# Attention heads on TensorE: the next head's probabilities are turned in front of the last head's products with the values

## The reference, cut to what matters

```
o_cmp = einsum('bgrqc,bgcd->bgrqd', p_cmp, v_cmp)              # compressed keys
o_slc = einsum('bgrqk,bgqkd->bgrqd', p_s, vs...)               # selected blocks
p_w   = safe_softmax(where(mask_w, s_w, -inf))
o_win = einsum('bgrqk,bgkd->bgrqd', p_w, vw)                   # window
return gb[..., 0:1] * o_cmp + gb[..., 1:2] * o_slc + gb[..., 2:3] * o_win
```

## Time and profile before

| what | value |
|---|---|
| median of 3 timed runs | 1402.15 us (1400.98 to 1402.82) |
| profiled execution | 1403.39 us, its span 1401.6 us |
| TensorE busy | 1336.2 us (95%) |
| VectorE busy | 787.1 us (56%) |
| ScalarE busy | 660.6 us (47%) |
| GpSimd busy | 39.5 us (3%) |
| HBM read and written | 429.40 MB and 1.05 MB |

### The profile page before, as it was taken

One profiled execution on the slowest core, in us unless ns is written; L12 is line 12 of the kernel. 1 busy time (PEld: TensorE's weight loads), 2 busy tenths in 40 slices (PEclk: granted clock), 3 DMA queues, 4 the chain that ended last, 5 costly groups with the idle time before them and its releaser, 6 DMA issues.

```text
span 1401.6 us, 19436 instructions
## 1 busy us (share of the span) xinstructions
PE 1336.2 (95%) x7580; PEld 1003.3 (72%) x7580; DVE 787.1 (56%) x864; ACT 660.6 (47%) x772; POOL 39.5 (3%) x97
## 2 busy tenths in 40 slices
PE   7999999998998898999999999999999999999996
PEld 7987888887986676777676766676666667666652
DVE  6855655545856858874376643367644266744332
ACT  5546543435645746763365532356542256633221
POOL 7000000001000000000000000000000000000000
PEclk9999999999999989999999999999999999999999
DMA  8453555554642035999999989999999999999996
GB/s 345 155 177 109 197 197 187 180 181 150 205 174 103 1 112 220 341 368 422 421 421 421 421 321 421 421 420 421 421 373 422 420 420 421 421 359 421 421 421 285
DMA packets 59993, 431.70 MB, mean 308 GB/s; under 512 B 6656, under 2 KB 6656, under 8 KB 7808
## 3 DMA queue, kind: packets, MB, share of 16 engines
q1 hardware_dynamic: 59760, 429.95, 77.3%
q10 hardware_dynamic: 144, 0.52, 0.1%
HBM read 429.40 MB, written 1.05 MB: 307 GB/s over the span
## 4 chain that ended last, share of the span: by engine, by line
PE 78%; DMA 13%; DVE 4%; ACT 4%; issue 1%; POOL 0%; SPq 0%; POOLq 0%; DVEq 0%; ACTq 0%
PE bank L1553 19%; PE bank L1555 19%; PE bank L1554 19%; DMA raw<-in_moe 12%; PE bank L2061 6%; PE bank L2082 6%; PE bank L1929 2%; DVE w_lo L1458 1%; ACT w_hi L855 1%; PE bank L2008 1%; PE bank L2109 1%; PE bank L1912 1%; PE bank L1903 1%; DMA raw<-in_wts 1%; PE bank L2016 1%
## 5 line engine op out<-in xcount | busy, mean ns | idle before, releaser
L1458 DVE TENSOR_TENSOR w_lo<-raw,w_hi 128x2048 fp32r<-128x2048 f32 x130 | 295.8, 2290 | 235.7 <-ACT w_hi L855 235.4
L855 ACT ACTIVATE w_hi<-raw 128x2048 fp32r<-128x2048 f32 x130 | 248.1, 1918 | 255.4 <-DMA raw<-in_moe 222.8
L1553 PE MATMUL bank<-w_hi,ht_hi 128*128 128x512 f32 (+1 forms) x768 | 303.1, 395 | 0.9 <-DVE ht_lo L989 0.9
L1555 PE MATMUL bank<-w_hi,ht_lo 128*128 128x512 f32 (+1 forms) x768 | 296.9, 387 | 0.0
L1554 PE MATMUL bank<-w_lo,ht_hi 128*128 128x512 f32 (+1 forms) x664 | 255.8, 385 | 0.0
L957 DVE TENSOR_TENSOR w_lo<-raw,w_hi 128x2048 fp32r<-128x2048 f32 x73 | 166.7, 2290 | 110.5 <-ACT w_hi L531 110.3
L531 ACT ACTIVATE w_hi<-raw 128x2048 fp32r<-128x2048 f32 x74 | 141.5, 1919 | 95.8 <-PE bank L1555 92.9
L1553 PEld LDWEIGHTS bank<-w_hi,ht_hi 128*128 128x128 f32 x768 | 144.7, 188 | 44.8 <-issue 13.7
L1555 PEld LDWEIGHTS bank<-w_hi,ht_lo 128*128 128x128 f32 x768 | 144.6, 188 | 30.1
L2061 PE MATMUL bank<-raw,xb 128*64 128x256 f32 x1280 | 147.1, 381 | 0.0
L1554 PEld LDWEIGHTS bank<-w_lo,ht_hi 128*128 128x128 f32 x664 | 125.2, 189 | 23.2
(11 more groups left out here) (339 smaller groups left out, 1568.5 us busy)
## 6 DMA issues: line engine op xcount, KB each, us to landing
raw<-in_moe SPq DMA_DIRECT2D x247, 1024.0 KB, 15.0
more<-in_moe SPq DMA_DIRECT2D x89, 1024.0 KB, 16.1
raw<-in_wts SPq DMA_DIRECT2D x71, 1024.0 KB, 4.8
xs<-in_x SPq DMA_DIRECT2D x2, 512.0 KB, 4.0
out<-xn SPq DMA_DIRECT2D x4, 256.0 KB, 2.0
pk<-in_packed SPq DMA_DIRECT2D x1, 517.0 KB, 8.4
g1b<-in_norm_ffn ACTq DMA_DIRECT2D x1, 512.0 KB, 6.0
gfb<-in_norm_final SPq DMA_DIRECT2D x1, 512.0 KB, 20.1
```

What stands on the lines that cost most here:

```text
L855: a(w_hi[:, hi_order(n) % SPLIT, :], slot_raw(n), ACT.Copy).then_inc(s_hi, 1)
L1458: v.tensor_tensor(slot_lo(n), slot_raw(n), w_hi[:, hi_order(n) % SPLIT, :].bitcast(F32), ALU.subtract).then_inc(s_lo, 1)
L1553: mm(out_, sh, mh, start=first, stop=False)
L1555: return mm(out_, sl, mh, start=False, stop=last)
```

## The change

In every step n the call of `head_transpose(n)` goes from behind `head_out(n - 1)` to in front of it. No instruction is added or taken away, and ScalarE's and VectorE's lists stay as they are.

```diff
         for n in range(2 * HB):
             if n % 2 == 0 and 4 <= n + 2 < 2 * HB:
                 pair_scores(n + 2)
+            head_transpose(n)
             if n:
                 head_out(n - 1)
-            head_transpose(n)
             if n % 2 == 0 and n >= 4:
                 pair_turned((n - 4) // 2)
         head_out(2 * HB - 1)
```

## The result

The changed kernel takes 1388.1 us (1386.9 to 1389.0, 4 runs) against 1401.89 of the kernel before beside it. The ratio is 0.9901, with a 95% interval from 0.9884 to 0.9918. The forecast was 1393.9, the range 1391.0 to 1397.5: faster, as forecast, but by 13.8 us instead of 8.3.

The account below looks back on a forecast made before the run. TensorE was taken to bound wide steps through its wait for ScalarE's copy, a VectorE-ScalarE ring narrow ones. 0.44 + 4.9 + 0 + 0.67 + 1.5 + 0.8 = 8.3 us off 1402.15 gave 1393.9 us, range 1391.0 to 1397.5.

Parts of the forecast that it names:

- first step: Products of step 0 wait for copied values; the turn of step 1 now lies in that wait: gain 0.44 us.
- wide even steps: Wide pairs fall from 5.00 to 4.30 us as the copy is hidden: 7 x 0.70 = 4.9 us.
- narrow steps: Gain 0 us: a ring without TensorE sets the pace, 3.03 us a pair or 4.11 with the splits.
- entry at step 24: Entry into the ring with the splits: step 24's copy no longer waits for its turn, gain 0.67 us.
- small ones: Remainder at changes between wide and narrow steps, between 0 and 1.5 us, taken as 0.8.
- last steps: From step 29's products on, two copies and the turn of step 30 leave the path: 1.5 us.
- the ring: VectorE and ScalarE, without TensorE, set the pace in narrow steps: 3.03 us a pair, 4.11 with the splits.
- The rule on weight loads: Loads pulled past a waiting instruction would cost 0.8 us of gain in all; the trace shows none.
- rivals 1, 3 and 4: Ring binds wide steps, 1397.0 us (0.17); turn delays coefficients, 1407.5 (0.03); waits replaced or already overlapped, 1402 (0.04).
- The clock: TensorE's clock, 0.51 from 492.50 to 500.50 us before, was expected to fall again, at an unknown place.
- Rival 2: Clock stays up in the last steps and projection: 10.7 us gain, 1391.5 us; chance 0.14.
- Carried to the end: Behind the loop, the expert weight stream starts earlier by the same amount, so the gain counts in full.

Follow-up runs that it names:

- first comparison: The changed kernel (every turn in front of the products) against the kernel before: 1388.1 us against 1401.89, ratio 0.9901.
- no_copy_wait: Kernel before, but products of step n read step n - 1's turned probabilities and wait for that copy alone: loop 60.40 us, whole 1608 us.
- narrow_only: Changed kernel with the turn in front of the products in narrow steps alone: 1395.8 us, ratio 0.9978 to the kernel before, loop 65.79 us.
- second comparison: The same changed kernel and kernel before, both unedited, measured again: 1388.9 us against 1399.3, ratio 0.9932.
- split_behind: Changed kernel with the two halves of the weight slot split behind the loop: 1385.4 us, ratio 0.9911 to the kernel before, loop 55.72 us.
- before_split_behind: Kernel before with the two halves of the weight slot split behind the loop: 1392.9 us, ratio 0.9962 to the unedited one, loop 64.58 us.

## Why the prediction was wrong

The main mechanism held: the copies left TensorE's path. The size was too small by 2.1 us in the loop, by two terms of the sum, and behind the second of them stands a bound that I had read wrongly. The first comparison added 3.4 us that aren't in the loop. Those put the time below the range: with the loop's 10.4 us alone it would have been 1391.8 us, inside it.

| step, as predicted | predicted | measured in the loop |
|---|---|---|
| first step | 0.44 | 0.45 |
| wide even steps | 7 x 0.70 = 4.9 | 1.00 + 0.89 + 1.02 - 0.02 + 0.90 + 0.88 + 0.99 = 5.7 |
| narrow steps | 0 | 0.06 a pair within a stretch, counted in the next row |
| entry at step 24, and small ones | 0.67 + 0.8 | 0.80 + 0.19 + 0.05 + 0.49 + 0.81 + 0.17 = 2.5 |
| last steps | 1.5 | 1.74 |
| sum | 8.3 | 10.4 |

(The measured ones are the differences of the distances between the scores of one pair and the next.)

- *Wide even steps* is a failed term. TensorE's own time in a pair is 4.10 us, not 4.30. I corrected the drain and the turned rows by estimates; what I missed is that products that wait pay for their weight load in full afterwards (0.11 us), shown by no_copy_wait, and 0.06 of order. The last 0.03 are within my estimate of the drain. One of the seven steps, 16, gave nothing: its turn waits 0.48 us for exponentials in the changed kernel, and the chain that ended last reaches it through the ring. So the term was wrong by 0.2 a pair and one pair too many.
- *The rule on weight loads* I turned the wrong way round, as something that could take from the gain. In the changed kernel the load at 436.67 us starts 0.11 us ahead of its matmul; in the kernel before the load at 440.90 us doesn't pass the waiting instruction. Together the two make the gain larger. The Trainium skill, "TensorE: Matmul & The Clock Gate", section "Step-by-step: what each phase is for", says that TensorE pulls weight loads ahead of running matmuls; the row at 436.67 us agrees.
- *Small ones*, with the entry at step 24, is the other failed term: 1.5 us predicted, 2.5 measured. Its cause is a wrong reading: "in narrow steps TensorE isn't the bound". In the kernel before it was, with its uncovered copies, and their wait was no slack; what the change could take was the distance down to the ring. Inside the stretch this is 0.06 us a pair, so the 0 of the narrow term was nearly right by luck. At the changes of shape it is more: narrow_only alone gives 0.8 us in the first narrow stretch and 0.84 at step 24. I had taken the copy of step 11, which shows no idle time, for all copies; those of even steps had waited for their turn.
- *The ring* has 2.97 us in narrow pairs, near the 3.03 that I had read off TensorE's own period, and 4.10 us with the splits, where it did bind before (4.11). Right were also the statement that a turn can't hold its products back by more than its length, and that the coefficients' wait stays small (2.0 us). So rivals 1, 3 and 4 fell. (The 4.19 us of rival 1 was the distance at the change from narrow to wide; the next one, between wide pairs, was 4.99, and is 3.93 now.)
- *The clock* fell and came back as I forecast, at 0.51 for 7 us, 3.4 us less than before. The part inside the projection is nearly the same, 2.5 us and 2.3. Rival 2 didn't happen in the changed kernel, and happened as soon as the splits left the loop.
- *Carried to the end*: yes, as far as can be told. SyncE's next load came 12.64 us earlier at nearly the same distance from the projection, and the stretch behind the loop didn't grow.
- *The rest of the 13.8 us.* The profiled pair had 2.33 us ahead of the loop and 1.61 behind it. The unchanged kernel shows both lengths of the first, so it is scatter; the cause of the second stays open. I worked the range out from the loop alone, and left none of its width to the scatter of a comparison of three or four runs: the kernel before had medians of 1401.9, 1399.3, 1400.4 and 1398.3 us in the comparisons of this study. The interval of the second comparison, 7.0 to 11.9 us, holds the loop's 10.4 and my 8.3 alike; it is the loop, which repeats to 0.02 us, that shows the sum to be too small. What makes the first stretch vary by up to 5.9 us (first turn at 424.5 to 430.3 us) wasn't tried.

## What to carry to other kernels

In a chain from TensorE over a copy back to TensorE, put a neighbour's work of at least the copy's length between the two; here the products of another step (0.85 us) cover a copy of 0.65 us, and a turn of 0.44 doesn't. Count a wait by two marks, its idle time and the weight load that could not be pulled ahead of it. Before you call a wait slack because two engines have the same period, follow the chain through one period and look whether it ever reaches the other engine. Look at each change of shape in a loop by itself, since the difference between two bounds that nearly agree in the steady state can be large there. When the named engine is freed, read the ring of the other engines next, and move what isn't due yet out of it.

## What I had not expected of the hardware

TensorE's clock fell to 1.2 GHz near the end of the loop in all eleven traces with the split halves in steps 24 to 27. TensorE was busy there for 7.6 of 11.0 us before, with no single wait over 1.0 us ahead of the fall. After the change it was busy for 7.8 of 10.5, and the fall came within a wait of 1.93 us for exponentials that ended at 481.42. The clock stayed at 2.4 GHz in the three kernels without the halves, where TensorE was busy for 9.07 of 10.00 us in split_behind and for 7.96 of 10.00 in before_split_behind. In split_behind 2.3 us come from the ring, and another 1.8 us, nearly as much, I put down to the clock: 0.7 in the last steps and 1.1 at the start of the projection. Whether those 1.1 us reach the end can't be told from the scatter behind the loop.
